# The order of long and short matmuls in an MLP's up products

## The reference

```
def _sq_relu_mlp(h, w_up, w_down):
    u = jax.nn.relu(h @ w_up)
    return (u * u) @ w_down

x = x + _sq_relu_mlp(_rmsnorm(x, a_norm_mlp[i]), a_w_up[i], a_w_down[i])
```

## Time and profile before

| | us |
|---|---|
| median of 3 runs | 928.08 |
| runs | 926.46 to 929.03 |
| the profiled execution, its own time | 928.42 |
| its span, first to last instruction | 926.7 |
| TensorE matmuls busy in the span | 917.0 (99%) |
| VectorE, ScalarE busy | 574.1, 473.4 |

### The profile page before, as it was taken

The page is one execution under the profiler, slowest core; times in us unless marked ns, Lnnn a source line. Parts: engine busy times, 40 slices in busy tenths (PEclk is TensorE's granted clock), DMA queues, the critical chain, the costliest instruction groups (busy, mean ns, idle before and its releaser), DMA issues.

```text
span 926.7 us, 13209 instructions
## 1 busy us (share of the span) xinstructions
PE 917.0 (99%) x4740; PEld 768.6 (83%) x4740; DVE 574.1 (62%) x779; ACT 473.4 (51%) x718; POOL 55.2 (6%) x126
## 2 busy tenths in 40 slices
PE   8999999999999999999999999999999999999998
PEld 7778788888888888788888888888887888888886
DVE  4768658655555668365855655677886555444453
ACT  5866557444444566654644444556456463444441
POOL 1202121000000000000200000002130010000000
PEclk9999999999999999999999999999999999999999
DMA  8945135655556534234755555455613255556541
GB/s 290 334 137 165 65 137 196 222 196 201 184 182 191 171 137 136 92 113 147 262 188 198 199 186 183 152 174 179 197 63 128 92 181 182 181 183 197 189 155 46
DMA packets 95435, 157.77 MB, mean 170 GB/s; under 512 B 5928, under 2 KB 37624, under 8 KB 95392
## 3 DMA queue, kind: packets, MB, share of 16 engines
q1 hardware_dynamic: 93824, 155.08, 50.1%
q10 hardware_dynamic: 1536, 2.11, 0.7%
q0 software_dynamic: 32, 0.02, 0.0%
HBM read 156.12 MB, written 1.06 MB: 170 GB/s over the span
## 4 chain that ended last, share of the span: by engine, by line
PE 96%; DVE 2%; issue 1%; ACT 1%; DMA 0%; ACTq 0%; POOL 0%
PE proj L1563 10%; PE proj L1565 10%; PE proj L1564 10%; PE score L1563 6%; PE score L1564 6%; PE score L1565 6%; PE outp L1565 6%; PE outp L1563 6%; PE outp L1564 6%; PE turn L1622 6%; PE proj L1622 6%; PE turn L1626 3%; PE proj L1626 3%; PE turn L1609 2%; PE outp L1812 2%; PE score L1774 2%
## 5 line engine op out<-in xcount | busy, mean ns | idle before, releaser
L1904 DVE TENSOR_TENSOR wlo<-raw,whi 128x2048 fp32r<-128x2048 f32 (+1 forms) x131 | 297.7, 2277 | 192.5 <-ACT whi L1331 147.6
L1331 ACT ACTIVATE whi<-raw 128x2048 fp32r<-128x2048 f32 x64 | 122.6, 1916 | 170.0 <-PE outp L1565 57.5
L1563 PE MATMUL proj<-whi,set 128*128 128x512 f32 (+1 forms) x428 | 169.5, 396 | 1.0 <-DVE set L2069 1.0
L1565 PE MATMUL proj<-whi,set 128*128 128x512 f32 (+1 forms) x428 | 165.7, 387 | 0.0
L1564 PE MATMUL proj<-wlo,set 128*128 128x512 f32 (+1 forms) x428 | 165.2, 386 | 0.0
L1320 ACT ACTIVATE whi<-raw 128x2048 fp32r<-128x2048 f32 (+1 forms) x67 | 126.7, 1897 | 51.4 <-PE outp L1565 17.2
L1563 PEld LDWEIGHTS proj<-whi,set 128*128 128x128 f32 x428 | 80.4, 188 | 17.9 <-issue 1.7
L1565 PEld LDWEIGHTS proj<-whi,set 128*128 128x128 f32 x428 | 80.3, 188 | 16.8
L1564 PEld LDWEIGHTS proj<-wlo,set 128*128 128x128 f32 x428 | 80.5, 188 | 14.9
L1563 PE MATMUL score<-whi,set 128*128 128x512 f32 x236 | 92.9, 393 | 0.0
L1563 PE MATMUL outp<-whi,set 128*128 128x512 f32 x236 | 92.4, 391 | 0.0
(11 more groups left out here) (228 smaller groups left out, 1171.9 us busy)
## 6 DMA issues: line engine op xcount, KB each, us to landing
raw<-in_a_w_up SPq DMA_DIRECT2D x32, 512.0 KB, 4.2
raw<-in_a_w_down SPq DMA_DIRECT2D x32, 512.0 KB, 4.2
raw<-in_b_w_up SPq DMA_DIRECT2D x32, 512.0 KB, 4.2
raw<-in_b_w_down SPq DMA_DIRECT2D x32, 512.0 KB, 4.6
raw<-in_w_gate SPq DMA_DIRECT2D x22, 512.0 KB, 4.0
raw<-in_w_up SPq DMA_DIRECT2D x22, 512.0 KB, 5.0
raw<-in_w_down SPq DMA_DIRECT2D x22, 512.0 KB, 4.1
raw<-in_a_w_in SPq DMA_DIRECT2D x20, 512.0 KB, 7.1
```

The lines of the kernel that those rows point to most:

```text
L1331: act.activation(shaped(whi, u), shaped(raw, u), ACT.Copy).then_inc(hi_done, 1)
L1563: pe.matmul(out_, hi, wh, start=start, stop=False)
L1565: return pe.matmul(out_, lo, wh, start=False, stop=stop)
L1904: return dve.tensor_tensor(shaped(wlo, u)[:, ks, :], shaped(raw, u)[:, ks, :], shaped(whi, u)[:, ks, :], ALU.subtract)
```

## The change

In `up_pair`, the second pair of loops goes away, and its product stands in the first pair of loops. Before, a call issued eight long products (both column blocks) and then eight short ones. After it, each long product of a (i, k) is followed at once by the short product of the same (i, k). The instructions, their operands, the start and stop flags and the semaphore step are the same; the values are added into a bank in another order.

```
--- before.py
+++ after.py
@@ -1620,9 +1620,6 @@
                     for k in range(UK):
                         moving = sets[hset][:, UK * h + k, :, :].rearrange("p s n -> p (s n)")
                         pe.matmul(pair[:, i, :], wh[:, k, cols], moving, start=h == 0 and k == 0, stop=False)
-                for i in range(2):
-                    cols = slice((2 * q + i) * P, (2 * q + i + 1) * P)
-                    for k in range(UK):
                         ins = pe.matmul(pair[:, i, 0:TOK], wl[:, k, cols], set_hi[hset][:, UK * h + k, :],
                                         start=False, stop=h == 1 and k == UK - 1)
                 ins.then_inc(mul_done, 1)
```

## The result

The changed kernel takes 930.38 us (median of 22 runs, 928.59 to 931.48), the kernel before 926.67 us in 22 runs (926.13 to 929.03). The ratio is 1.003, with an interval of 1.0024 to 1.0037: slower by 0.3%, or 2.8 us. I had forecast -0.1%. The runs of either kernel fall into two groups some 2 us apart, and the medians lie in different groups, so their difference of 3.7 us says too much: group against group it is 2.6 us (926.3 to 928.9) and 2.3 us (928.2 to 930.5). Ahead of the MLPs the kernels differ by as much as these groups: in the profiled executions of this study the first up product starts anywhere from 142.2 to 145.5 us.

The account below looks back on a forecast made before the run. TensorE's matmul stream was taken to bound the kernel, busy 99%. 512 pairs at 0.3470 in place of 0.3484 us give -0.7 us, so 927.4 us as a median; range 923.9 to 931.9 us.

Parts of the forecast that it names:

- The chain stayed on TensorE: Sign in one loop pass: chain on TensorE, idle 0.0 before L1622, clock 1.00, no wait in the loop.
- The arithmetic from pair to kernel: Up products: 32 pairs a chunk, 16 chunks; 0.347 for 0.3484 us a pair gives -0.7 us.
- their count: Weight loads under the up products: eight under short and eight under long products in either order, so little-cover loads unchanged.
- One reading of the cover: Bank T in the loop: written again only next pass, 22.05 us after 225.41, so shifts of tens of nanoseconds are covered.
- the sum: Up products: long behind short 0.233 plus short behind long 0.114 give 0.347 us a pair, -0.7 us in all.
- start-up cost: Product behind the block (L1563) still follows a short one and keeps this cost; settling sooner would give 0.5 us at most.
- the fast rival: Up products: long product needs only 0.227, not 0.233; pair 0.341, kernel 924.3 us; chance 0.20.
- The slow rival: Up products: stream never settles, every long product 0.236, every short 0.120; +3.9 us, kernel 932.0 us; chance 0.17.
- The threshold where it decides: Up products: the rival of a never-settling stream decides from a pair of 0.354 us.
- The case "nothing": Up products: prices of neighbours cancel, 0.348 us a pair, kernel 928.1 us; chance 0.13.
- the forecast's price: Up products in the new order: 0.347 us for one long and one short product; forecast's chance 0.50.

Follow-up runs that it names:

- the experiment with 384 columns: Changed kernel with the short product lengthened from 256 to 384 columns: up products of a pass 13.00 us, 0.4063 a pair.
- runs of two: Changed kernel reordered to two long products, then two short ones: 11.14 us for a pass's up products, ratio 1.0001 to the kernel before.
- runs of four: Changed kernel reordered to four long products, then their four short ones: 11.20 us for a pass's up products, ratio 1.0011 to the kernel before.

## Why the prediction was wrong

**What held.** The chain stayed on TensorE, without waits in the six passes, at full clock, and the change is worth only what the distances are worth. The arithmetic from pair to kernel held too: 0.353 a pair is +0.14 us a pass, as seen. That the loads are no part of it, as I argued from their count, fits the quick pattern; the experiment with 384 columns gives the load more cover and finds no gain, but does not clear it alone. One reading of the cover was loose: TensorE also adds to bank T in the fourth call of the same pass, from 231.00. The cover that counts runs from VectorE's sum at 234.62 to the next pass at 247.46, some 12 us, and was still ample.

**The step that failed** is the sum: "The nearest rows are 0.233 and 0.114. They give 0.347 for a pair". I took the long product's price from one right behind a run of eight short ones and the short product's from the first behind eight settled long ones, and supposed that both would stand together in every pair. The measured pair in the loop is 0.3533 us: the long product takes 0.236 on average (its durations are 395, 398 and 403 ns, so 0.233 to 0.241 by the settled 389 ns at 0.227), and the short one 0.117 (277, 281 and 284 ns, where 278 went with 0.114 and 283 with 0.120). So each of the two was some 3 ns too low. Both of my prices do occur in the slow pattern, but each in one pair of three. A second, smaller term failed too: I let the down products keep their start-up cost, and they take 10.95 us in place of 10.91, which is 0.4 to 0.5 us of the growth by 2.0.

The rows for this were in front of me: in the kernel before, the first long products behind short ones do not fall back to 0.227 at once, but pass through larger distances over some five products (233, 236, 228, 233 and 230 ns). I even used that, as an argument against the fast rival, and not against my own sum.

**The rivals.** The slow rival named the mechanism, a stream that never settles, with the long product at 0.236, exactly as measured; its 0.120 for the short one was 3 ns too high, so that it gave +3.9 us, and the trace has +2.0 and the timed ratio +2.8. The threshold where it decides, 0.354 a pair, was just not reached in the trace; by time the kernel is slower by 0.30%. The fast rival is out: no pattern shows 0.227 behind a short product. The case "nothing" is out as well: the same 64 products take 11.09 to 11.29 us by their order and by the pattern that they fall into. The Trainium skill (page "TensorE: Matmul & The Clock Gate", section "Back-to-back issue gap") gives N/2.4 + 2.5 ns as the gap of an isolated warm matmul, which my forecast left out, and about 131 ns for 512 columns in a stream of loads and products. Neither number has a term for the neighbours, and neither agrees with these runs, where products of 512 columns with a load each settle at 226.7 ns. Its section "LDWEIGHTS (loading the stationary operand)" gives for a load of 128 columns, worked out from its formula as an estimate, 107 ns; the rows of the loads here last 187 to 192 ns. Either number would make the load under a short product a suspect; the quick pattern speaks against it.

**What I gave the forecast's price** did exist, in the stretch behind the transposes (0.3468) and in the loop with transposes ahead (0.3466). That it comes to my 0.347 is luck: the pattern is not 0.233 + 0.114 but 0.230 + 0.117. The stream has several steady patterns, and I had priced it as if it had one.

**What stays open.** Why the slow pattern costs more than the settled distances is not shown; nor how the state of the stream picks a pattern, nor why runs of two cost less than runs of four. The runs leave little room for the change of weight buffer (no cost at 512 columns), for the operands and the half of the bank (no change in the loop), for waits (none), and for the cover of the load. Of the 2.8 us of the timed ratio (2.2 to 3.4) the two traces show 2.0; the rest isn't placed. And two corrections to the description above: the loop runs over five passes, not six, with one pass before and one behind it; and TensorE waits on `up_added` before both calls of h = 0, not the first alone.

## What to carry to other kernels

When TensorE is busy all the time, the order of matmuls of different lengths can still be worth something, here up to 0.2 us in 11, and it shows only in the distance from start to start, not in the busy share. Don't add up the prices of single neighbours: a regular stream settles into a pattern, and the pattern's sum is what is paid. Take a price from a row right behind a disturbance only if you know how long the disturbance lasts, and ask whether the new order ever lets it end.

## What the runs showed that I had not expected

One instruction stream has steady patterns at two prices, 0.3533 and 0.3467 us a pair, that last as long as it does: 32 pairs in the loop and 56 behind the transposes. The lower price is the sum of the two settled distances, so strict alternation can be free. What stands ahead matters, since eight transposes took thirteen of fourteen passes to the lower price, but the instructions do not decide it: the same calls behind the same transposes ran at either price in the two MLPs of one execution, and the one difference found that goes with it is whether the products some thirty places ahead had settled. Runs of two (11.14 us) are cheaper than runs of four (11.20 us), though the length changes twice as often.
